# Diagonal products of an experts' mix on four 64x64 tiles of the array

## The reference

```python
q = (xf @ lp['peer_wq']).reshape(n, PEER_HEADS, 2, PEER_HALF)          # 8 heads, 2 halves
sub = jnp.einsum('nhpd,hpkd->nhpk', q, lp['peer_keys'])                 # 128 keys per half
top_s, top_i = lax.top_k(sub, PEER_TOPK)                                # 16 of each half
best_s, best_pos = lax.top_k(cand_s, PEER_TOPK)                         # 16 of the 256 sums
gate = jax.nn.softmax(best_s, axis=-1)                                  # idx, gate: (n, 128)
act = jax.nn.gelu(jnp.einsum('ted,td->te', lp['peer_u'][ib], xb), approximate=False)
out = jnp.einsum('te,ted->td', gb * act, lp['peer_v'][ib])
x = x + out; y = rmsnorm(x, final_norm_w)
```

## Time and profile before

| | |
|---|---|
| median of 3 runs | 4407.8 us (4405.5 to 4409.2) |
| span of the profiled execution, first to last instruction | 4396.6 us |
| TensorE busy | 3822.2 us, 87% |
| VectorE / ScalarE / GpSimd busy | 2494.4 / 1311.1 / 1375.8 us |
| gathers' queue (software_dynamic) | 1082.2 MB of 1316.6 |
| matmuls of `mix`, L2731 | 1920.4 us in 4096 records |
| mean granted TensorE clock | 0.948 of full speed |

### The profile page before, as it was taken

One profiled execution on the slowest core, in us unless ns is written; L12 is line 12 of the kernel. 1 busy time (PEld: TensorE's weight loads), 2 busy tenths in 40 slices (PEclk: granted clock), 3 DMA queues, 4 the chain that ended last, 5 costly groups with the idle time before them and its releaser, 6 DMA issues.

```text
span 4396.6 us, 41856 instructions
## 1 busy us (share of the span) xinstructions
PE 3822.2 (87%) x11589; PEld 1968.3 (45%) x11589; DVE 2494.4 (57%) x5467; ACT 1311.1 (30%) x3882; POOL 1375.8 (31%) x1240
## 2 busy tenths in 40 slices
PE   8988889997888799898899998889999888877876
PEld 4555245553542455443445543445554344433432
DVE  2333356555112677554677754677755567766664
ACT  2332133331001233242332342233333233333332
POOL 0000033330000333454433443433344343334443
PEclk9997899997988899999999999999999999999999
DMA  6001000005413899999999999999999999999997
GB/s 213 29 33 46 21 15 19 14 14 203 183 39 144 345 418 418 420 417 421 420 401 406 418 421 420 420 389 413 412 420 412 421 419 404 419 419 400 420 420 291
DMA packets 227214, 1316.58 MB, mean 299 GB/s; under 512 B 27208, under 2 KB 43501, under 8 KB 93328
## 3 DMA queue, kind: packets, MB, share of 16 engines
q0 software_dynamic: 148608, 1082.20, 59.5%
q1 hardware_dynamic: 77256, 232.11, 14.0%
q10 hardware_dynamic: 1152, 0.00, 0.0%
HBM read 1283.71 MB, written 32.68 MB: 299 GB/s over the span
## 4 chain that ended last, share of the span: by engine, by line
DMA 27%; PE 26%; DVE 7%; issue 3%; ACT 2%; DVEq 1%; ACTq 0%; POOL 0%; POOLq 0%
DMA ex_ring<-in_expert_uv,ex_idx 26%; PE psum L2731 17%; DVE ex_ring L3116 4%; PE psum L2760 4%; PE psum L2709 3%; ACT ex_diag L2912 1%; PE psum L2779 1%; PE psum L2804 0%; DMA ex_ring<-in_expert_uv,ex_idxT 0%; ACT ex_weight L2907 0%; PE psum L2821 0%; POOL ex_ring L2651 0%; DMA pair_p<-scratch_mixed 0%; DVE ex_best_at L3042 0%; ACT ex_dots L2903 0%
## 5 line engine op out<-in xcount | busy, mean ns | idle before, releaser
L2731 PE MATMUL psum<-ex_ring,ex_diag 128*128 128x512 f32 x4096 | 1920.4, 613 | 331.1 <-ACT ex_diag L2912 309.9
L3116 DVE CUSTOM_DVE_ANT_0 ex_ring<-ex_ring,ex_x_rows 128x1024 f32<-128x1024 f32 x1024 | 1250.5, 1226 | 826.8 <-DMA ex_ring<-in_expert_uv,ex_idx 756.1
L2651 POOL DMA_INDIRECT ex_ring<-in_expert_uv,ex_idx x1024 | 1159.5, 1132 | 1731.2 <-PE psum L2731 1528.3
L2731 PEld LDWEIGHTS psum<-ex_ring,ex_diag 128*128 128x128 f32 x4096 | 773.4, 195 | 1301.7 <-issue 849.0
L2903 ACT ACTIVATE ex_dots<-ex_dots 128x2 f32<-128x2 f32 x512 | 104.1, 203 | 1795.4 <-DVEq L3119 1795.0
L2912 ACT ACTIVATE ex_diag<-ident,ex_weight 128x128 f32<-128x128 f32 x1024 | 355.1, 394 | 36.7 <-issue 1.7
L1122 PE MATMUL psum<-w_zx,ssd_hT 128*128 128x512 f32 (+1 forms) x768 | 295.3, 541 | 7.6 <-DMA ssd_hT<-scratch_hT 6.9
L2709 PE MATMUL psum<-ex_xT,ex_chunk 128*128 128x256 f32 (+1 forms) x1280 | 276.6, 360 | 4.2 <-ACT ex_sub L2888 2.9
L2709 PEld LDWEIGHTS psum<-ex_xT,ex_chunk 128*128 128x128 f32 x1280 | 229.2, 191 | 97.3 <-issue 77.0
L2907 ACT ACTIVATE ex_weight<-ex_gates,ex_dots 128x1 f32<-128x1 f32 x1024 | 245.9, 287 | 36.8 <-issue 1.7
L1122 PEld LDWEIGHTS psum<-w_zx,ssd_hT 128*128 128x128 f32 x768 | 137.5, 192 | 161.8 <-issue 154.0
(11 more groups left out here) (449 smaller groups left out, 3695.8 us busy)
## 6 DMA issues: line engine op xcount, KB each, us to landing
ex_chunk<-in_route_wq SPq DMA_DIRECT2D x80, 512.0 KB, 8.0
ex_chunk<-in_w_out SPq DMA_DIRECT2D x48, 512.0 KB, 9.0
ex_ring<-in_expert_uv,ex_idx POOLq DMA_INDIRECT x1024, 20.3
ex_chunk<-in_read_wq SPq DMA_DIRECT2D x24, 512.0 KB, 8.0
ex_chunk<-in_w_mo SPq DMA_DIRECT2D x24, 512.0 KB, 7.9
w_zx<-in_w_in SPq DMA_DIRECT2D x1, 10304.0 KB, 35.0
w_out<-in_w_out SPq DMA_DIRECT2D x2, 4096.0 KB
w_out<-in_cache_mem_k SPq DMA_DIRECT2D x8, 1024.0 KB, 11.1
```

The lines of the kernel that those rows point to most:

```text
L2651: nc.gpsimd.indirect_dma_start(out=ring[:, n % RING, :], out_offset=None, in_=io["expert_uv"], in_offset=bass.IndirectOffsetOnAxis(ap=idx[ ...
L2731: ins = nc.tensor.matmul(psum[c][:], diag[:, q % 3, s, :], ring[:, n % RING, D + c * BANK:D + (c + 1) * BANK], start=(n % SLOTS == 0), sto ...
L3116: nc.vector.tensor_tensor_reduce(ring[:, n % RING, 0:D], ring[:, n % RING, 0:D], x_rows[:, tile % 3, :], 1.0, 0.0, ALU.mult, ALU.add, dots ...
```

## The change

The diagonal product of a slot is written as four matmuls in place of two. Token half r (partitions 64r to 64r + 63 of ring and diagonal) and column half c of the value row give a product with 64 rows and 64 columns of the array, 512 moving columns, written to partitions 64c to 64c + 63 of bank r. The order is (0,0), (1,1), (0,1), (1,0). The stationary operand is now 128x64: two 64x64 diagonals one above the other, made from `unit`, the sum of the identity's two column halves.

So the result of a tile lies in quarters: partition 64c + i, bank r, column j holds token 64r + i, value 512c + j. Residual, gain and result take the same layout: two DMAs in place of one for each load and store (`quarters`), a gain of 512 columns, and a mean of squares that adds the lower and the upper 64 partitions (`averaged`). The 8 sample rows keep rows of 1024; their gain is loaded into 8 partitions of `gain_ffn` when its last other use is over.

```diff
-        res, junk = sb("ex_res", [P, D]), sb("ex_junk", [P, BANK])
-        gain, gain_ffn = sb("ex_gain", [P, D]), sb("ex_gain_ffn", [P, D])
+        res, junk = sb("ex_res", [P, 2, BANK]), sb("ex_junk", [P, BANK])
+        gain, gain_ffn = sb("ex_gain", [P, BANK]), sb("ex_gain_ffn", [P, D])
+        gain_own = gain_ffn[0:DEC, :]
...
-        diag = sb("ex_diag", [P, 3, SET, P])
-        ms, mean, rstd, minus_half = sb("ex_ms", [P, 2]), sb("ex_mean", [P, 1]), sb("ex_rstd", [P, 1]), sb("ex_minus_half", [P, 2])
+        diag, unit = sb("ex_diag", [P, 3, SET, HP]), sb("ex_unit", [P, HP])
+        ms, mean, rstd, minus_half = sb("ex_ms", [P, 2]), sb("ex_mean", [P, 2]), sb("ex_rstd", [P, 2]), sb("ex_minus_half", [P, 2])
+        upper, both = sb("ex_upper", [HP, 2]), sb("ex_both", [P, 2])
...
+            def quarters(name, tile):
+                return io[name][tile * P:(tile + 1) * P, :].rearrange("(r i) (c j) -> c i r j", r=2, c=2)
             def load_res(tile):
                 if tile:
-                    sp.wait_ge(stored, 16 * tile)
+                    sp.wait_ge(stored, 32 * tile)
                 if tile >= GT:
                     sp.wait_ge(x2_stored, 32 * (tile // GT))
-                sp.dma_start(res[:], io["x2"][tile * P:(tile + 1) * P, :]).then_inc(res_in, 16)
+                for c in range(2):
+                    sp.dma_start(res[c * HP:(c + 1) * HP, :, :], quarters("x2", tile)[c]).then_inc(res_in, 16)
             def store(tile):
                 sp.wait_ge(out_ready, tile + 1)
-                sp.dma_start(io["y_prompt"][tile * P:(tile + 1) * P, :], res[:]).then_inc(stored, 16)
+                for c in range(2):
+                    sp.dma_start(quarters("y_prompt", tile)[c], res[c * HP:(c + 1) * HP, :, :]).then_inc(stored, 16)
...
-            sp.dma_start(gain[:], io["final_norm_w"].broadcast_to([P, D])).then_inc(gain_in, 16)
+            for c in range(2):
+                sp.dma_start(gain[c * HP:(c + 1) * HP, :], io["final_norm_w"][:, c * BANK:(c + 1) * BANK].broadcast_to([HP, BANK])).then_inc(gain_in, 16)
...
                     sp.dma_start(own_sum, io["x2"][SEQ:TOKENS, :]).then_inc(own_res_in, 16)
+                    sp.wait_ge(xn_ready, GT * (GROUPS - 1))
+                    sp.dma_start(gain_own, io["final_norm_w"].broadcast_to([DEC, D])).then_inc(gain_own_in, 16)
...
-                nc.gpsimd.tensor_tensor(rstd[:], mean[:], minus_half[:, 0:1], ALU.pow).then_inc(rstd_ready, 1)
+                nc.gpsimd.tensor_tensor(rstd[:], mean[:], minus_half[:], ALU.pow).then_inc(rstd_ready, 1)
...
-                    for c in range(2):
-                        ins = nc.tensor.matmul(psum[c][:], diag[:, q % 3, s, :], ring[:, n % RING, D + c * BANK:D + (c + 1) * BANK],
+                    for r, c in ((0, 0), (1, 1), (0, 1), (1, 0)):
+                        half = slice(r * HP, (r + 1) * HP)
+                        ins = nc.tensor.matmul(psum[r][c * HP:(c + 1) * HP, :], diag[half, q % 3, s, :],
+                                               ring[half, n % RING, D + c * BANK:D + (c + 1) * BANK],
                                                start=(n % SLOTS == 0), stop=(n % SLOTS == SLOTS - 1), skip_group_check=True)
                     ins.then_inc(mixed, 1)
...
-                    ins = nc.scalar.activation(diag[:, q % 3, s, :], ident[:], ACT.Copy, scale=weight[:, q % 2, s:s + 1])
+                    ins = nc.scalar.activation(diag[:, q % 3, s, :], unit[:], ACT.Copy, scale=weight[:, q % 2, s:s + 1])
...
-                    nc.scalar.activation(junk[:], res[:, c * BANK:(c + 1) * BANK], ACT.Square, accum_out=ms[:, c:c + 1])
+                    nc.scalar.activation(junk[:], res[:, c, :], ACT.Square, accum_out=ms[:, c:c + 1])
...
-                dve.wait_ge(res_in, 16 * (tile + 1))
-                for c in range(2):
-                    cols = slice(c * BANK, (c + 1) * BANK)
-                    ins = nc.vector.tensor_tensor(res[:, cols], psum[c][:], res[:, cols], ALU.add)
+                dve.wait_ge(res_in, 32 * (tile + 1))
+                for r in range(2):
+                    ins = nc.vector.tensor_tensor(res[:, r, :], psum[r][:], res[:, r, :], ALU.add)
                 ins.then_inc(summed, 1)
...
-                nc.vector.tensor_tensor(ms[:, 0:1], ms[:, 0:1], ms[:, 1:2], ALU.add)
-                dve.drain()
-                nc.vector.tensor_scalar(mean[:], ms[:, 0:1], 1.0 / D, EPS, ALU.mult, ALU.add).then_inc(mean_ready, 1)
+                nc.vector.tensor_copy(upper[:], ms[HP:P, :])
+                dve.drain()
+                nc.vector.tensor_tensor(both[0:HP, :], ms[0:HP, :], upper[:], ALU.add)
+                dve.drain()
+                nc.vector.tensor_copy(both[HP:P, :], both[0:HP, :])
+                dve.drain()
+                nc.vector.tensor_scalar(mean[:], both[:], 1.0 / D, EPS, ALU.mult, ALU.add).then_inc(mean_ready, 1)
+            def averaged_own():
+                dve.wait_ge(ms_ready, TILES + 1)
+                dve.wait_ge(rstd_ready, TILES)
+                nc.vector.tensor_tensor(ms[0:DEC, 0:1], ms[0:DEC, 0:1], ms[0:DEC, 1:2], ALU.add)
+                dve.drain()
+                nc.vector.tensor_scalar(mean[0:DEC, 0:1], ms[0:DEC, 0:1], 1.0 / D, EPS, ALU.mult, ALU.add).then_inc(mean_ready, 1)
...
-                nc.vector.scalar_tensor_tensor(res[:], res[:], rstd[:], gain[:], ALU.mult, ALU.mult).then_inc(out_ready, 1)
+                for r in range(2):
+                    ins = nc.vector.scalar_tensor_tensor(res[:, r, :], res[:, r, :], rstd[:, r:r + 1], gain[:], ALU.mult, ALU.mult)
+                ins.then_inc(out_ready, 1)
...
-                nc.vector.scalar_tensor_tensor(own_sum, own_sum, rstd[0:DEC], gain[0:DEC, :], ALU.mult, ALU.mult).then_inc(out_ready, 1)
-
+                dve.wait_ge(gain_own_in, 16)
+                nc.vector.scalar_tensor_tensor(own_sum, own_sum, rstd[0:DEC, 0:1], gain_own, ALU.mult, ALU.mult).then_inc(out_ready, 1)
...
+            nc.vector.tensor_tensor(unit[:], ident[:, 0:HP], ident[:, HP:P], ALU.add).then_inc(unit_ready, 1)
             dve.wait_ge(count_ready, 1)
-            dve.wait_ge(gain_in, 32)
+            dve.wait_ge(gain_in, 48)
...
-            averaged(TILES)
+            averaged_own()
```

8 lines of the change are left out of this document (5 added, 3 removed).

## The result

| | before | after |
|---|---|---|
| median of 5 runs each | 4405.5 us (4401.6 to 4409.2) | 4423.7 us (4421.3 to 4425.6) |
| span of the profiled execution | 4396.6 us | 4419.2 us |
| TensorE busy | 3822.2 us | 3316.3 us |
| mean granted TensorE clock | 0.948 | 0.874 |

What follows compares the result with a forecast made beforehand. The prediction took the transfers as the bound, TensorE close behind and bound together with them in the read stretches. Its +95 us for TensorE, other terms 0, gave a 4491.6 us span, or 4503 us beside the median, range 4385 to 4620.

Steps and rivals of the forecast that it cites:

- What bounds the kernel: Experts' mix, 1477 to 4362 us: transfers are the bound, TensorE close behind; a faster TensorE could win at most 41 us.
- step 3: TensorE in the crowded read stretches: 0.85 us more per turn, 109 us too much work less 14 caught up, +95 us.
- 11.2 us: Difference between the profiled span, 4396.6 us, and the runs' median, 4407.8 us, taken to lie around the span and left alone.
- Step 1: Overlap of the mix's sixteen quarter-array records on TensorE: between 1.72 and 6.88 us a turn, taken as 3.87 against 3.44.
- ordered pairs: Mix on TensorE: a matmul's second record waits for its first and holds up the next quarter; 3.87 us a turn, chance 0.56.
- Rival A: Mix on TensorE: all four quarters run together, 1.72 us plus 0.42 a turn; -15 us, 4393 us; chance 0.24.
- Step 2: TensorE between the mix and other matmuls: changing tile size costs 0.42 us in each turn with other work between mixes.
- Step 4: ACT's 1024 diagonals, 128 to 64 columns: about 340 ns each in place of 394, hidden by the transfers, 0 us.
- Step 5: Residual, result and gain in quarters, with rows of 2 KB in place of 4 KB: 0 us, bound 0 to 20.
- Step 6: Means of squares on DVE: four small operations in place of two, under 0.7 us nine times, hidden, 0 us.
- C: Mix on TensorE: no overlap, tiles run one by one, 6.88 us plus 0.42 a turn; +1440 to +1475 us, 5870; chance 0.20.

Runs made afterwards that it cites:

- before_6k: The kernel before with the u half of each gathered row cut to 512 values, 6 KB in place of 8 KB; 4021.4 us.
- direct_6k: direct with the u half of each gathered row cut to 512 values, rows of 6 KB; 3799.3 us, 222 us less than before_6k.
- ragged: direct with the four products of a slot 512, 480, 448 and 416 columns wide, so widths name the tiles; a single run took 4403 us.
- two_tiles: The whole sum in the layout of the kernel before, on only two 64x64 tiles, rows and columns 0 to 63 and 64 to 127; 4415.5 us, ratio 1.0018.
- half_parts: The kernel before with each tile's residual loaded by two DMAs of 64 partitions each, whole rows of 4 KB; 4421.6 us, ratio 1.0032.
- half_cols: The kernel before with each residual loaded by two DMAs over all 128 partitions, one per column half, rows of 2 KB; 4408.7 us, ratio 0.9999.
- after_again: The changed kernel once more, unaltered, measured in the experiments' series against the kernel before; 4422.4 us, ratio 1.0033.
- direct: The changed kernel's four tiles with residual, store, gain and mean as before the change; VectorE adds the residual in four pieces; 4408.9 us, ratio 1.0004.

## Why the prediction was right and wrong

*What bounds the kernel.* Right: the transfers, with TensorE close behind. before_6k and direct_6k show both halves of it. The sentence that a TensorE which does more "is paid for almost fully" is wrong; see step 3. The 11.2 us "around the span" are wrong too. A run's time is 1.8 to 2.1 us over its span in every run here. The rest is mostly the start of the program, which varies from one execution to the next before any changed line: the last product of attention's projection (L320) begins at 367.0 us in before's trace, at 376.1 in after's and at 379.7 at the latest, in before_6k's.

*Step 1, overlap,* is the step that failed. It took the middle mechanism, ordered pairs, 9T = 3.87 us. The mix takes 1.95 us, and ragged shows why: each tile has its own sequence, in which its two records follow each other, and none waits for another tile's. Rival A's mechanism was the true one; its 1.72 us are 1.95 with the last record's end after its stream. The choice between the two mechanisms went by a rule of order that no row showed, and that does not hold for these records.

*Step 2, change of tile size,* was sized about right: 0.42 us forecast, 0.34 in two_tiles' crowded turn. With four tiles it is covered.

*Step 3, the sum on TensorE,* +95 us, falls with step 1. It also had a fault of its own. two_tiles lengthens the crowded turns by 0.34 us; this step's counting makes that 31 us too much, and 8 were paid. What a stretch of 300 us held too much was largely made up in the stretch behind it. So even with ordered pairs the +95 would have been too high.

*Step 4, ACT:* 340 ns forecast, 340 ns measured, no effect.

*Step 5, residual in quarters,* is the term that makes the slowdown, and the second that failed. It was put at 0 by the size of the rows (2 us if short pieces were a tenth worse), with bounds of 0 to 20. It measures +12.9 us in half_parts, against +15 to +18 for the whole change. The bound held, the reason did not: half_cols has the same rows of 2 KB at no cost. What counts is that each load writes to one half of the partitions, beside the gathers, which write all 128. It was also said to be hidden under a TensorE bound; there was none. The place of the chunk loads on SP and the sample's gain showed no effect.

*Step 6, the small operations:* four of 152 to 169 ns in place of two, no effect. The end takes 4.1 us longer in after's trace, but only 1.6 in after_again's, and 3.2 in direct's, which has the means of before. Over all traces with rows of 8 KB the end takes 38.0 to 39.3 us with the old products and 39.6 to 42.3 with tiles, so some 2 us go with the tiles; why was not looked for.

*The rivals.* A was right in its mechanism and wrong in its gain: direct, which is A without the new layout, is at +0.1 us by its median (0.9995 to 1.0013), not -15. The slow moments of the transfers were neither TensorE's fault nor did they go when TensorE had time. What A allowed for, that the granted clock would fall and the longer mix be hidden, happened: 0.81 to 0.95 by stretch, and mixes of 3.45 to 3.69 us in lone turns. C, +1440 us, has nothing for it: the array runs the tiles together.

The sign of the forecast came from the wrong term, and that it was right is luck. The 4503 was the sum of an effect that the four tiles do not have (+95) and a zero that should have been +13.

## What to carry to other kernels

Before pricing a faster engine, ask what the bound resource would do with it: here 525 us less of TensorE's busy time gained some 3 us in the stage and nothing in the median, and with gathered rows lighter by a quarter the same edit gave 222 us. When a faster operation forces a new layout, price the transfers of the new layout first, by which partitions each of them writes and by its outermost dimension, not by bytes and row length alone. In two_tiles 8 of 31 us were paid for stretches that were too full for TensorE; the stretches behind them made up the rest. So such an excess is not to be added up as it stands.
